# Attention keys and values of three tiles kept in SBUF, in place of one U slot and two V slots of the gather rings

## The reference, cut to what matters

```python
# stick-breaking attention, a block of 128 queries against all keys
z = jnp.einsum('bhtd,bhsd->bhts', qb, kh)
lneg = jnp.where(mask, jax.nn.log_sigmoid(-z), 0.0)
rexcl = lax.cumsum(lneg, axis=3, reverse=True) - lneg
A = jnp.where(mask, jnp.exp(jax.nn.log_sigmoid(z) + rexcl), 0.0)
o = jnp.einsum('bhts,bhsd->bhtd', A, vh)
...
# experts: per token 8 heads x 16 chosen rows of two tables of 16384 x 1024
eidx = jnp.take_along_axis(cidx, fi, axis=-1)
ue = expert_u[eidx]
ve = expert_v[eidx]
act = jax.nn.gelu(jnp.einsum('td,thkd->thk', xt, ue), approximate=False)
return jnp.einsum('thk,thkd->td', g * act, ve)
```

## Time and profile before

| | us |
|---|---|
| median of 3 runs | 3272.96 |
| lowest, highest run | 3268.18, 3273.04 |
| profiled execution | 3272.3 |
| its span | 3270.4 |

### The profile page before, as it was taken

The page is one execution under the profiler, slowest core; times in us unless marked ns, Lnnn a source line. Parts: engine busy times, 40 slices in busy tenths (PEclk is TensorE's granted clock), DMA queues, the critical chain, the costliest instruction groups (busy, mean ns, idle before and its releaser), DMA issues.

```text
span 3270.4 us, 32739 instructions
## 1 busy us (share of the span) xinstructions
PE 2102.9 (64%) x10776; PEld 1108.5 (34%) x10776; DVE 2207.6 (68%) x5532; ACT 627.6 (19%) x1358; POOL 1941.5 (59%) x2079
## 2 busy tenths in 40 slices
PE   8999996564576456645675467646864578444443
PEld 6777854221232123312332134213521244111110
DVE  4454437766776677766876687768776778766663
ACT  1121113110221113111321133102311133100000
POOL 0000005767776767666676766676677667777775
PEclk9999997776777668867877688767886689766666
DMA  6211239999999999999999999999999999999998
GB/s 208 72 39 52 82 150 341 409 407 409 409 408 408 409 396 408 409 405 393 403 409 407 409 389 392 408 409 408 369 408 409 409 374 408 409 409 410 409 409 322
DMA packets 339473, 1160.62 MB, mean 355 GB/s; under 512 B 36004, under 2 KB 50024, under 8 KB 338280
## 3 DMA queue, kind: packets, MB, share of 16 engines
q0 software_dynamic: 294912, 1073.87, 82.8%
q1 hardware_dynamic: 44392, 84.65, 7.2%
HBM read 1140.54 MB, written 17.84 MB: 354 GB/s over the span
## 4 chain that ended last, share of the span: by engine, by line
DMA 39%; PE 28%; DVE 15%; POOL 11%; issue 7%; ACT 1%; DVEq 0%; POOLq 0%; ACTq 0%
DMA work<-expert_u,chosen 22%; DMA work<-expert_v,idx_v 17%; PE xs L1449 11%; PE acc L1449 8%; DVE work L1331 7%; POOL work L644 5%; POOL work L627 5%; PE xs_ahead L1449 5%; PE bank L1449 4%; DVE work L961 1%; DVE work L953 1%; DVE rest L1231 1%; DVE cand L953 1%; DVE work L958 1%; DVE sri L1230 0%
## 5 line engine op out<-in xcount | busy, mean ns | idle before, releaser
L1331 DVE CUSTOM_DVE_ANT_0 work<-work,xs 128x1024 f32<-128x1024 f32 x1003 | 1220.1, 1220 | 589.6 <-DMA work<-expert_u,chosen 557.1
L627 POOL DMA_INDIRECT work<-expert_u,chosen x1024 | 968.5, 946 | 850.6 <-DVE chosen L961 471.6
L644 POOL DMA_INDIRECT work<-expert_v,idx_v x1024 | 968.0, 945 | 461.3 <-issue 260.7
L1449 PE MATMUL acc<-work,lw 128*32 128x512 f32 x4096 | 756.8, 877 | 709.0 <-DMA work<-expert_v,idx_v 702.0
L1449 PEld LDWEIGHTS acc<-work,lw 128*32 128x32 f32 x4096 | 139.1, 139 | 1084.4 <-DMA work<-expert_v,idx_v 571.0
L1449 PE MATMUL bank<-weights,n2T 128*128 128x256 f32 x1024 | 261.4, 412 | 0.0
L1449 PEld LDWEIGHTS bank<-weights,n2T 128*128 128x128 f32 x1024 | 207.5, 209 | 121.2 <-issue 92.6
L1449 PE MATMUL xs<-work,weights 128*128 128x128 f32 x1664 | 193.1, 277 | 0.0
L1449 PEld LDWEIGHTS xs<-work,weights 128*128 128x128 f32 x1664 | 189.4, 193 | 1.4 <-issue 1.3
L1449 PE MATMUL xs<-weights,work 128*128 128x512 f32 x416 | 187.1, 605 | 0.0
L1449 PE MATMUL xs_ahead<-work,neg_tri 128*128 128x512 f32 x176 | 123.6, 791 | 88.6 <-DVE work L961 63.1
(11 more groups left out here) (201 smaller groups left out, 2351.6 us busy)
## 6 DMA issues: line engine op xcount, KB each, us to landing
work<-kv_dram SPq DMA_DIRECT2D x88, 256.0 KB, 6.4
work<-expert_u,chosen POOLq DMA_INDIRECT x1024, 14.1
work<-expert_v,idx_v POOLq DMA_INDIRECT x1024
weights<-w_in SPq DMA_DIRECT2D x6, 2048.0 KB, 17.3
mix_dram<-work SPq DMA_DIRECT2D x8, 1024.0 KB, 4.0
weights<-w_queryT SPq DMA_DIRECT2D x4, 2048.0 KB, 7.8
work<-xT SPq DMA_DIRECT2D x9, 512.0 KB, 7.1
kv_dram<-work SPq DMA_DIRECT2D x9, 512.0 KB, 5.9
```

Of the source, the lines that this page charges most:

```text
L627: pool.indirect_dma_start(out=ring_u[:, s, :], out_offset=None, in_=expert_u, in_offset=bass.IndirectOffsetOnAxis(ap=chosen[:, G % KEPT_HE ...
L644: pool.indirect_dma_start(out=ring_v[:, e % RING_V, :], out_offset=None, in_=expert_v, in_offset=bass.IndirectOffsetOnAxis(ap=idx_v[:, G % ...
L1331: nc.vector.tensor_tensor_reduce(s, s, rows[:, :, :].rearrange("p a b -> p (a b)"), 1.0, 0.0, ALU.mult, ALU.add, dots[:, col:col + 1]).the ...
L1449: return nc.tensor.matmul(out_, lhsT, rhs, start=start, stop=stop, skip_group_check=True)
```

## The change

`RING_U` becomes 6 and `RING_V` 8. The room goes to `kept[0]` and `kept[1]`, keys and values of tiles 1 and 2 (512 KB each), and to `lead_k` and `lead_v`, those of tile 0's 16 tokens. Each of them is loaded once (`load_kept`): tile 0 and 1 in the projections, tile 2 at the start of the second phase. Units of tiles 0 to 2 take their keys and values from there (`keys_of`, `vals_of`), and only the units with M - i >= 3 are loaded by `load_kv`. In the unit of tile 0 (`i == T`) all steps work on 16 partitions in place of 128, and its `add_later` is left out, since no unit follows. With `RING_V` 8 the wait of V gather e is (e - 8) // 4 + 1 sets: all four gathers of set n need the sum of set n - 2.

```diff
-RING_U = 7
+RING_U = 6
-RING_V = 10
+RING_V = 8
+KEPT = 3
...
+def streamed(T, i):
+    return sum(max(t - KEPT + 1, 0) for t in range(T)) + i
+def stream_end(T):
+    while T > 0 and T < KEPT:
+        T -= 1
+    return units_before(T) + T - KEPT + 1 if T >= KEPT else 0
...
+        kept = [sb(f"kept{i}", [P, 2 * MIX]) for i in range(1, KEPT)]
+        lead_k = sb("lead_k", [P, SHP, N_META])
+        lead_v = sb("lead_v", [N_META, SH, SD])
...
             def load_kv(T, i):
-                c = units_before(T) + i
+                c, e = units_before(T) + i, streamed(T, i)
+                done = c if i > 0 else stream_end(T - 1)
-                wait(sp, z_done, 2 * c)
+                wait(sp, z_done, 2 * done)
                 sp.dma_start(keys, ...).then_inc(k_in, 16)
-                wait(sp, av_done, c)
+                wait(sp, av_done, done)
                 sp.dma_start(vals, ...).then_inc(v_in, 16)
+            def load_kept(j):
+                if j == 0:
+                    sp.dma_start(lead_k[:, :, :], kv_dram[0][:, 0:MIX].rearrange("p (c s) -> p c s", c=SHP)[
+                        :, :, P - N_META:P]).then_inc(kept_in[0], 16)
+                    sp.dma_start(lead_v[:, :, :], kv_dram[0][P - N_META:P, MIX:2 * MIX].rearrange(
+                        "p (h d) -> p h d", h=SH)).then_inc(kept_in[0], 16)
+                else:
+                    sp.dma_start(kept[j - 1][:, :], kv_dram[j]).then_inc(kept_in[j], 16)
...
                     for i in range(1, M + 1):
-                        load_kv(M, i)
+                        if M - i >= KEPT:
+                            load_kv(M, i)
...
-                    last = STT(sp_[hg], bank[4 + hg][:, :], 0.0, zl[hg], ALU.max, ALU.add)
+                    m = n_keys(T, i)
+                    last = STT(sp_[hg][0:m, :], bank[4 + hg][0:m, :], 0.0, zl[hg][0:m, :], ALU.max, ALU.add)
...
             def add_later(T, i):
                 dve.wait_ge(s_done, 2 * c + 2)
                 dve.wait_ge(sp_ready, 2 * c + 2)
+                if i == T:
+                    dve.sem_inc(later_ready, 1)
+                    return
...
             def z(T, i):
-                pe.wait_ge(k_in, 16 * (c + 1))
+                if T - i >= KEPT:
+                    pe.wait_ge(k_in, 16 * (streamed(T, i) + 1))
+                else:
+                    pe.wait_ge(kept_in[T - i], 32 if i == T else 16)
```

More of the change, by code:

```diff
@@ L388, in program @@
         k_in, v_in = sem("k_in"), sem("v_in")
+        kept_in = [sem(f"kept_in{i}") for i in range(KEPT)]
         z_done, ln_ready, sp_ready, s_done, later_ready, a_ready, av_done = (
@@ L430, in program, with keys_of, vals_of, n_keys @@
         SLOT = {"c": 0, "v": 1, "so": 2, "qs": 3, "ks": 4, "vs": 5}
+        def keys_of(T, i):
+            j = T - i
+            if j == 0:
+                return lead_k
+            return kept[j - 1][:, 0:MIX].rearrange("p (c s) -> p c s", c=SHP) if j < KEPT else keys
+        def vals_of(T, i):
+            j = T - i
+            if j == 0:
+                return lead_v
+            return kept[j - 1][:, MIX:2 * MIX].rearrange("p (h d) -> p h d", h=SH) if j < KEPT else vals
+        def n_keys(T, i):
+            return N_META if i == T else P
         def slot(p, name):
@@ L540, in _ @@
                     load_mix(1)
-                    load_kv(1, 0)
-                if T == 3:
-                    load_kv(1, 1)
+                    load_kept(0)
+                    if KEPT > 1:
+                        load_kept(1)
+                    else:
+                        load_kv(1, 0)
                 if T == 4:
@@ L563, in _ @@
             load_mix(2)
-            load_kv(2, 0)
+            if KEPT > 2:
+                load_kept(2)
+            else:
+                load_kv(2, 0)
             for T in range(1, LAST + 2):
@@ L791, in ln_z @@
                 wait(act, av_done, c)
+                m = n_keys(T, i)
                 for hg in range(2):
                     act.wait_ge(z_done, 2 * c + hg + 1)
-                    last = nc.scalar.activation(zl[hg], bank[4 + hg][:, :], ACT.Abs)
+                    last = nc.scalar.activation(zl[hg][0:m, :], bank[4 + hg][0:m, :], ACT.Abs)
                 Ls(last)
                 for hg in range(2):
-                    last = nc.scalar.activation(zl[hg], zl[hg], ACT.Exp, scale=-1.0)
+                    last = nc.scalar.activation(zl[hg][0:m, :], zl[hg][0:m, :], ACT.Exp, scale=-1.0)
                 Ls(last)
                 for hg in range(2):
-                    nc.scalar.activation(zl[hg], zl[hg], ACT.Ln, bias=one[:, :]).then_inc(ln_ready, 1)
+                    nc.scalar.activation(zl[hg][0:m, :], zl[hg][0:m, :], ACT.Ln, bias=one[0:m, :]).then_inc(ln_ready, 1)
             def exp_a(T, i):
@@ L808, in exp_a @@
                     act.wait_ge(sp_ready, 2 * c + hg + 1)
-                    nc.scalar.activation(zl[hg], bank[4 + hg][:, :], ACT.Exp).then_inc(a_ready, 1)
+                    m = n_keys(T, i)
+                    nc.scalar.activation(zl[hg][0:m, :], bank[4 + hg][0:m, :], ACT.Exp).then_inc(a_ready, 1)
             def square_o(T):
@@ L1607, in z @@
                     for cc in range(SHP):
-                        last = mm(bank[4 + hg][:, cc * P:(cc + 1) * P], keys[r, cc, :], qsT[r, cc, :], cc == 0,
+                        last = mm(bank[4 + hg][0:m, cc * P:(cc + 1) * P], keys_of(T, i)[r, cc, :], qsT[r, cc, :], cc == 0,
                                   False)
@@ L1617, in s @@
                     pe.wait_ge(sp_ready, 2 * c + hg + 1)
-                    b = bank[4 + hg][:, :]
-                    last = mm(b, neg_tri[:, :], sp_[hg], False, False)
+                    m = n_keys(T, i)
+                    b = bank[4 + hg][0:m, :]
+                    last = mm(b, neg_tri[0:m, 0:m], sp_[hg][0:m, :], False, False)
                     if diagonal(i):
@@ L1624, in s @@
                             pe.wait_ge(later_ready, c)
-                        last = mm(b, ones[:, :], later[hg], False, True)
+                        last = mm(b, ones[:, 0:m], later[hg], False, True)
                     last.then_inc(s_done, 1)
@@ L1634, in av @@
                         h = 2 * cc + hg
-                        last = mm(bank[6][:, h * SD:(h + 1) * SD], zl[hg][:, cc * P:(cc + 1) * P], vals[:, h, :],
+                        last = mm(bank[6][:, h * SD:(h + 1) * SD], zl[hg][0:m, cc * P:(cc + 1) * P],
+                                  vals_of(T, i)[0:m, h, :],
                                   diagonal(i) and h == 0, True)
```

11 lines of the change are left out of this document (9 added, 2 removed).

## The result

The changed kernel takes **3280.5 us** (median of 11 runs), the kernel before 3272.4 on the same occasion: 8 us more by the medians. The ratio is 1.0033, with a 95% interval of 1.0025 to 1.0041, which is about 11 us. I had forecast 3265 us, 8 us faster, in a range of 3253 to 3277, and had given slower a chance of 0.12. The forecast was wrong in its sign and in its range. The profiled execution has a span of 3282.0 us, 11.6 more than before; at 3283.8 us it is the slowest of the eleven, so its profile shows some 3 us more than the median run has.

What follows compares the result with a forecast made beforehand. From about 530 us on, bytes at 409 GB/s were taken to set the time. The terms -26 + 5.1 + 5.1 + 1.4 + 3.6 + 2.2 made -8.6, taken as -8: 3265 us, range 3253 to 3277.

Steps and rivals of the forecast that it cites:

- Bytes, -26: Key and value loads: 10.5 MB less at 409 GB/s, 25.6 to 28.3 us, taken as 26 us saved.
- Slots, +17.4 in five terms: Smaller rings where PE is late: tiles 7 and 8 5.1 us each, tile 6 1.4, start 3.6, end 2.2.
- The end, +2.2: Last four V gathers wait for the sum two sets before; the last lands at 3261.4 instead of 3259.20, 2.2 us.
- the 4.4 for an empty queue: Gather queues: landing time of a gather in an empty queue, taken as 4.4 us between bounds 3.8 and 5.7.
- Quiet stretches, 0: Stretches without attention: landings fall from 14 to about 9 us, 4.5 us of reserve is left, cost 0.
- a sign of being wrong: Quiet stretch: the prediction would be wrong if the rate there fell under 409 GB/s.
- the 8.9 us of the sum: Quiet stretches with eight V slots: 12.8 - 3.9 = 8.9 us from a gather's issue to its landing.
- The narrow unit, 0: Unit of tile 0: ACT and DVE on 16 partitions in place of 128 take the same time, no cost.
- Work taken away: Tile 0's unit: 10 us of running-sum updates leave DVE, none on the path; 16 partitions take the same time.
- The rival on the other side: Heads of tiles 3 to 8, middles of 3 to 5: lost pairs cost 23 us, so 3288 us; chance 0.12.

Runs made afterwards that it cites:

- slots alone: The kernel before with 6 slots of U and 8 of V, every key and value still loaded: 3292.0 us, +20.8 (ratio 1.0062).
- wide kernel: The changed kernel with the unit of tile 0 over 128 rows, on tile 1's kept keys and values, `add_later` back: 3269.0 us against 3270.4 before (0.9997).
- bytes alone: The kernel before with all 17 slots, loads of tiles 0, 1 and 2 left out from tile 3 on: 3243.7 us, -27.5 (0.9919).
- 5 and 9: The changed kernel with 5 slots of U and 9 of V, three tiles kept, tile 0 in 128 rows: 3257.9 us against 3270.2 before (0.9966).
- the kernel with 5 and 10 slots: 5 slots of U, 10 of V, tiles 0 and 1 kept in 128 rows, against the kernel before: 1.0119, at 365 GB/s only.

## Why the prediction was wrong

- **Bytes, -26: right.** Alone they measured -27.5 (an interval of -32 to -21), though of the 28.9 us in that kernel's profile 4.0 lie before the first dot, where no load is left out. In tiles 3 and 4 the changed kernel is 4.7 and 3.7 us shorter, 3.8 a tile being three units at 409 GB/s.
- **Slots, +17.4 in five terms: the sum right within the interval, the places right but three of them priced too low.** Alone they measured +20.8, an interval of +15 to +26. By the table (slots alone less before): tile 7 +4.7 and tile 8 +4.1, where I had 5.1 each; tile 6 +4.0, where I had 1.4; tile 5 +2.0, where I had none; tile 2's stretch, which begins with the start, +4.4, where I had 3.6; the end +5.5, where I had 2.2. What tile 6, tile 5 and the end cost more is about 8 us; tiles 3, 4 and the last stretch took 1.2 less.
- **The end, +2.2: mis-sized.** It is +6.1. In the changed kernel the last four V gathers are issued from 3260.70 to 3264.42 us and their sum starts at 3270.46, 6.0 us after the last issue. I had counted 4.4 us from the bounds of the earlier trace rows. They also start 1.9 us later against the last dot than I had worked out, and the last sum takes 3.64 us in place of 3.25. So of the 3.9 us missed the 4.4 for an empty queue explains 1.6. The same 4.4 is too short at 2385.90, where the U row behind a 5.35 us wait is waited for until 2392.75, 6.9 us; there a V gather issued 1.25 us earlier shares the queue.
- **Quiet stretches, 0: right in time.** The last stretch went from 329.8 to 329.2 us. By its letter a sign of being wrong came true, since three of its slices stand at 405 to 407 GB/s in place of 409, but it cost nothing. With 14 slots the landing time of U there is near the 8.9 us of the sum (wide kernel, 2897 to 3190 us; none is known for the changed kernel itself):

```profile
DMA to landing us min/median/max: 8.3/9.1/10.5
```

- **The narrow unit, 0: this is the step that failed.** Under "Work taken away" I priced it at nothing: of `add_later` I wrote "Nothing of it lies on the path", of ACT and DVE that they take the same time on 16 partitions. The latter holds: `make_sp` took 1.29 us on 16 partitions and 1.30 on 128, the logarithms on ACT 1.33 in both. PE's four matmuls by the triangle and the ones I left out without a reason. In tile 7, behind a wait of 3.9 us they run at half clock, in both kernels; with 16 inner rows in the triangle the clock is back only 10.0 us after the first of them, with 128 after 3.1; the set of sums behind them ends 3.4 us later (10.5 in place of 7.1 us after the first of them), and GpSimd waits for that very set, with too little in the queues to cover it. Measured for the whole unit: 11.7 us (ratios) or 12.9 us (table, tile 8's unexplained 1.6 included); about 10 us stand at the unit itself in tiles 5 to 7. It decides the sign: with 128 rows the kernel is level with the one before.
- **The rival on the other side** (reserve missed at every tile, 3288) isn't what happened. Tile heads lose nothing: tiles 3 and 4 kept the whole gain. Its reason, that a queue refills only slowly at 2.48 against 2.56 us a pair, tempted me again as theory I, and one run refuted that.
- **What stays open.** Slots alone plus bytes alone make -6.7, the wide kernel measured -1.4. The intervals of the three ratios, 3 to 6 us each way, leave room for no interaction as for one of 5 us. In tile 8 the wide kernel is 2.6 us slower than the two halves make, and GpSimd waits 4.37 us there just before the unit of tile 0, so a small one is possible. And whether the narrow unit costs anything with all slots and loads wasn't measured at 409 GB/s, nor was the width apart from `add_later`.

## What to carry to other kernels

Work that shrinks can still cost time: before a matmul is made smaller, look in the timeline whether it stands behind a wait, what the granted clock is there, and who waits for what runs next. Of two rings fed in turn by one engine, read which of the two waits is the longer, and take slots from the other: the same 14 slots were worth 10 us more as 5 and 9 than as 6 and 8. And when a kernel gives two things up for one, measure the halves: it was their sum, right to 2 us, that showed that the cause lay in neither.

## What the runs showed of the hardware

- **The granted clock came back later with matmuls of 16 inner rows, though PE was busy.** In tile 7 PE was busy for 10.04 of 10.20 us, all at half; with 128 rows it was at half for 3.4 us, and with these four matmuls alone at full size for 6.8 (at 365 GB/s, where the narrow unit had 13.7). In tiles 5 to 7 of all profiles it was back 9.3 to 17.3 us after the first of them with 16 inner rows, and at most 6.2 us after it with 128. Where the clock was at full as these matmuls began, in tile 8 at 409 GB/s, it stayed there. 128 output columns instead of 16 made no difference (9.94 of 10.20 us busy, half all the while).
- **A matmul's own time doesn't fall with its inner rows:** at half clock and with 128 output columns a pair by the triangle took 2.07 us with 16 inner rows and 2.07 or 2.08 with 128; with 16 columns it took 1.88.
- **Gathers issued together behind a wait land later than the shortest landing.** A U row was there 6.9 us after its issue, and the last set of V 6.0 us after its last gather, where the fastest U gather at the start of the second phase landed in 5.7.
- **The same kernel took 3270 us on some occasions and 3569 to 3592 on others**, at 409 and at about 365 GB/s. What cost 0.6% and what gained 0.8% at 409 GB/s measured within 0.2% of before at 365; the kernel with 5 and 10 slots cost 1.2% there.
